# Hybrid encoder on one core: VectorE's order within an attention tile, the modulation's row sums in the mixer's tail, and the order of the first loads

## What is computed

```python
mod = silu(c) @ w_ada[l] + b_ada[l]                    # six vectors of 1024
h = rms_norm(x, norm1_g) * (1 + sc1) + sh1
za, zb, zq, zk, zv = split(h @ w_in)
ya = silu(rms_norm(depthwise_conv31(val(za) * sigmoid(gate(za))) + b))
yb = rms_norm(bg * depthwise_conv3(cg * hv))           # from zb
w = softmax(q1 k1) - lam * softmax(q2 k2);  yc = rms_norm(w @ v) * (1 - lambda_init)
x = x + g1 * (concat(ya, yb, yc) @ w_out)
h = rms_norm(x, norm2_g) * (1 + sc2) + sh2
x = x + g2 * (silu(h @ w_gate) * (h @ w_up)) @ w_down
```

## Time and profile before

| | |
|---|---|
| median of 3 runs | 1249.59 us (1248.78 to 1251.52) |
| the profiled execution's own time | 1248.77 us |
| its span in the trace | 1246.8 us |
| mean granted TensorE clock | 0.984 |
| PE busy | 1189.5 us, 95% |
| DVE busy | 730.5 us, 59% |
| ACT busy | 470.5 us, 38% |
| chain of waits, by engine | PE 70%, DVE 21%, ACT 4%, issue 4% |
| chain of waits, lines of VectorE | L908 (taps) 5%, L799 4%, L1004 1%, L989 1%, L844 1% |

### The profile page before, as it was taken

One profiled execution on the slowest core, in us unless ns is written; L12 is line 12 of the kernel. 1 busy time (PEld: TensorE's weight loads), 2 busy tenths in 40 slices (PEclk: granted clock), 3 DMA queues, 4 the chain that ended last, 5 costly groups with the idle time before them and its releaser, 6 DMA issues.

```text
span 1246.8 us, 14190 instructions
## 1 busy us (share of the span) xinstructions
PE 1189.5 (95%) x5080; PEld 926.1 (74%) x5080; DVE 730.5 (59%) x1032; ACT 470.5 (38%) x706; POOL 90.3 (7%) x163
## 2 busy tenths in 40 slices
PE   7999897969999999999989998989899999999998
PEld 5887543748888888888868875548688888888887
DVE  6889997886555533366665999645633333333331
ACT  5544657433332233322243345674422332232220
POOL 2402112201011000111000001000000000000000
PEclk9999998979999999999989999999999999999999
DMA  7742114655565322587422221203233223323332
GB/s 290 257 163 85 34 52 151 208 197 167 188 201 188 128 89 101 182 303 239 162 75 102 85 85 34 63 6 102 67 101 101 88 97 101 100 86 106 113 101 84
DMA packets 44328, 158.36 MB, mean 127 GB/s; under 512 B 5185, under 2 KB 5313, under 8 KB 44290
## 3 DMA queue, kind: packets, MB, share of 16 engines
q1 hardware_dynamic: 30386, 107.13, 25.5%
q0 software_dynamic: 13904, 50.73, 11.9%
HBM read 155.75 MB, written 2.10 MB: 127 GB/s over the span
## 4 chain that ended last, share of the span: by engine, by line
PE 70%; DVE 21%; ACT 4%; issue 4%; DMA 1%; POOL 0%; DVEq 0%; ACTq 0%; SPq 0%
PE ps L1234 20%; PE ps L1235 20%; PE ps L1236 20%; DVE uc L908 5%; DVE w_lo L799 4%; PE ps L1258 2%; DVE prob L1004 1%; PE ps L1442 1%; DVE neg_max L989 1%; DVE ada_ring_mid_b L844 1%; PE ps L1262 1%; DVE ta L975 1%; DVE tb L980 1%; DVE tn L970 1%; ACT prob L581 1%
## 5 line engine op out<-in xcount | busy, mean ns | idle before, releaser
L501 ACT ACTIVATE w_hi<-raw 128x1024 fp32r<-128x1024 f32 x196 | 207.8, 1060 | 577.2 <-PE ps L1236 492.5
L799 DVE TENSOR_TENSOR w_lo<-raw,w_hi 128x1024 fp32r<-128x1024 f32 x196 | 240.1, 1226 | 266.1 <-ACT w_hi L501 265.9
L1234 PE MATMUL ps<-h_hi,w_hi 128*128 128x512 f32 x848 | 334.4, 394 | 0.0
L1236 PE MATMUL ps<-h_lo,w_hi 128*128 128x512 f32 x848 | 330.4, 390 | 0.0
L1235 PE MATMUL ps<-h_hi,w_lo 128*128 128x512 f32 x848 | 330.2, 389 | 0.0
L1234 PEld LDWEIGHTS ps<-h_hi,w_hi 128*128 128x128 f32 x848 | 159.2, 188 | 48.2 <-issue 16.7
L1236 PEld LDWEIGHTS ps<-h_lo,w_hi 128*128 128x128 f32 x848 | 159.2, 188 | 33.4
L1235 PEld LDWEIGHTS ps<-h_hi,w_lo 128*128 128x128 f32 x848 | 159.3, 188 | 31.7
L1234 PE MATMUL ps<-gu_hi,w_hi 128*128 128x512 f32 x352 | 136.9, 389 | 0.0
L1235 PE MATMUL ps<-gu_hi,w_lo 128*128 128x512 f32 x352 | 136.9, 389 | 0.0
L1236 PE MATMUL ps<-gu_lo,w_hi 128*128 128x512 f32 x352 | 136.9, 389 | 0.0
(11 more groups left out here) (168 smaller groups left out, 1261.2 us busy)
## 6 DMA issues: line engine op xcount, KB each, us to landing
raw<-w_stream SPq DMA_DIRECT2D x196, 512.0 KB, 3.3
ada_ring_gu<-ada POOLq DMA_DIRECT2D x28, 512.0 KB, 4.3
ada_ring_late<-ada POOLq DMA_DIRECT2D x28, 512.0 KB, 4.9
ada_ring_first<-ada POOLq DMA_DIRECT2D x16, 512.0 KB, 5.8
ada_ring_mid_a<-ada POOLq DMA_DIRECT2D x12, 512.0 KB, 5.8
ada_ring_mid_b<-ada POOLq DMA_DIRECT2D x12, 512.0 KB, 4.9
xT<-x_t SPq DMA_DIRECT2D x4, 512.0 KB, 8.7
out_t<-xT SPq DMA_DIRECT2D x8, 256.0 KB, 4.3
```

The source lines that it names most:

```text
L501: act.activation(w_hi[:, u % RING, :], raw[:, u % RAW, :], ACT.Copy).then_inc(s_whi, 1)
L799: dve.tensor_tensor(w_lo[:, u % RING, :], raw[:, u % RAW, :], w_hi[:, u % RING, :].bitcast(F32), ALU.subtract).then_inc(s_wlo, 1)
L1234: pe.matmul(dst, whi, rhs[0][:, n, :], start=start, stop=False)
L1236: return pe.matmul(dst, whi, rhs[1][:, n, :], start=False, stop=stop)
```

## The change

VectorE's tile has another order: maxima of the next tile, mixing, one tap, the next tile's inverse, and then the other taps. Taps are given per tile and reach to tile 13 in both layers; the sums (50 and 26) are unchanged. In layer 0's tail the eight row sums 20 to 27 stand in pairs between the steps, where before four stood there and four behind; head 2's remainder (`y_lo(l, 3)`) is now ahead of the convolution's scaling (`mix_scale(l, 4)`), in both layers. GpSimd issues the loads 20 to 25 in pairs behind the factors of tiles 13, 14 and 15, where four came behind tile 13's and two behind tile 14's. At the start SyncE issues `pcol` after all of x, GpSimd's first two `ada` loads wait for the third load of x, ScalarE's first weight split comes ahead of the first gain, and VectorE's angle reduction and first weight remainder come ahead of the norm.

```diff
-TAPS_TILE = ([(1, 3)] * 10 + [(1, 4)] * 2, [(1, 3)] * 6 + [(2, 0)])
+TAPS_TILE = ((5, 4, 5, 3, 2, 4, 5, 3, 2, 3, 5, 3, 3, 3, 0, 0), (3, 2, 3, 1, 1, 2, 3, 1, 1, 1, 3, 1, 2, 2, 0, 0))
@@ SyncE
                 sp.dma_start(xT[:, 2 * i:2 * i + 2, :], x_in[:, 2 * i:2 * i + 2, :]).then_inc(s_x[i], 16)
-                if i == 1:
-                    sp.dma_start(pcol[:], pcol_in).then_inc(s_pc, 16)
+            sp.dma_start(pcol[:], pcol_in).then_inc(s_pc, 16)
@@ GpSimd, attention
-                    if l == 0 and it == N_TILES - 3:
+                    if l == 0 and it >= N_TILES - 3:
                         pool.wait_ge(s_scores, N_TILES)
-                        for m in range(M_MID + 4, M_MID + 8):
-                            ada_load(m)
-                    if l == 0 and it == N_TILES - 2:
-                        for m in range(M_MID + 8, M_MID + 10):
-                            pool.wait_ge(s_acc, m - 8 + 1)
+                        for m in range(M_MID + 2 * it - 22, M_MID + 2 * it - 20):
+                            if m >= M_MID + 8:
+                                pool.wait_ge(s_acc, m - 8 + 1)
                             ada_load(m)
@@ GpSimd, start
-            for m in range(2):
-                ada_load(m)
...
             pads()
+            pool.wait_ge(s_x[KC // 2 - 2], 16)
+            for m in range(2):
+                ada_load(m)
             pool.wait_ge(s_x[KC // 2 - 1], 16)
@@ ScalarE, start
             norm_rstd(0)
+            split_hi(0)
             act.wait_ge(s_pc, 16)
             act.wait_ge(s_n1b, 1)
             first_gain(0)
-            split_hi(0)
@@ VectorE, start
             angle_turns()
+            reduce_angles()
             dve.wait_ge(s_pc, 16)
...
             mod_dot(0)
             mod_dot(1)
-            reduce_angles()
+            split_lo(0)
             dve.wait_ge(s_nrs, 1)
...
                         norm_apply(0, 0, k)
-                        if k == 0:
-                            split_lo(0)
-                        elif k + 1 < KC:
+                        if k and k + 1 < KC:
                             mod_dot(2 * k + 2)
@@ VectorE, attention tile
-                    taps = TAPS_TILE[l][it] if it < len(TAPS_TILE[l]) else (0, 0)
-                    conv_a_taps(l, taps[0])
                     row_mix_in(l, it)
+                    taps = TAPS_TILE[l][it]
+                    conv_a_taps(l, min(taps, 1))
+                    if it + 1 < N_TILES:
+                        row_inverse(l, it + 1)
+                    conv_a_taps(l, taps - min(taps, 1))
                     if it in (3, 7):
                         short_input(l, it // 4)
                     if it in (9, 11):
                         short_gate(l, it // 2 - 4)
-                    conv_a_taps(l, taps[1])
-                    if it + 1 < N_TILES:
-                        row_inverse(l, it + 1)
@@ VectorE, tail
                 y_lo(l, 2)
-                mix_scale(l, 3)
-                mix_scale(l, 4)
-                y_lo(l, 3)
                 if l == 0:
                     for m in range(M_MID + 4, M_MID + 6):
                         mod_dot(m)
-                y_lo(l, 4)
+                mix_scale(l, 3)
                 if l == 0:
                     for m in range(M_MID + 6, M_MID + 8):
                         mod_dot(m)
+                y_lo(l, 3)
+                if l == 0:
+                    for m in range(M_MID + 8, M_MID + 10):
+                        mod_dot(m)
+                mix_scale(l, 4)
+                y_lo(l, 4)
+                if l == 0:
+                    for m in range(M_MID + 10, M_MID + 12):
+                        mod_dot(m)
                 mix_scale(l, 5)
                 y_lo(l, 5)
-                if l == 0:
-                    for m in range(M_MID + 8, M_MID + 12):
-                        mod_dot(m)
```

## The result

The changed kernel takes 1254.15 us (median of 15 runs, 1252.52 to 1258.77), the kernel before 1249.96 in as many. The ratio is 1.0035, with a 95% interval of 1.0027 to 1.0043: slower by 4.2 us by the medians (4.4 by the ratio), where +4.3 was forecast.

The account below looks back on a forecast made before the run. TensorE was taken to have most of the chain, VectorE the pace in four places. Terms 1.0 + 0 + 2.6 + 2.8 − 4.9 + 0.7 + 2.1 = +4.3 us on 1249.59 gave 1253.9, range 1249.0 to 1257.0.

Parts of the forecast that it names:

- start: First norm: the weight's first split and remainder delay the activations' remainder, +1.0 us, bounds 0 to +3.
- layer 0, tiles 0 to 11: Six taps fewer, −4.0 us, against twelve waits of 0.33 at the inverse, +4.0: sum 0.
- layer 0, tiles 12 and 13: Of three new taps one fits the inverse's wait, two lengthen each tile: +2.6 us.
- layer 0, tile 14: The mixing's 1.12 us wait for GpSimd goes, tile 15's inverse waits anyway: taken as 0, other end −1.1.
- layer 0, tail: Convolution's scaling held back, SiLU 4.4 us later, clock falls for 1.7; output units begin 2.8 us later.
- layer 1, tiles 0 to 11: Thinly spread taps leave TensorE's own pace of 4.51 or 5.35 us a tile: −4.9 us.
- layer 1, last tiles: Tile 12: one tap ahead of head 0's scaling, for which ScalarE waits, +0.7 us; tile 13 nothing.
- layer 1, tail: Convolution's scaling ends later than the SiLU's old start, all of it counting: +2.1 us.
- The second rival: Layer 0's tiles: no wait at the inverse, 14 × 0.33 us less; total −0.3, 1249.3 us; chance 0.13.
- The first rival: Both tails: scaling not held, row sums leave VectorE's path; total −3.9, 1245.7 us; chance 0.14.
- I take 0: Layer 1's tail: clock's price behind TensorE's gap of 3.0 us, left open at 0 to +1.7, taken as 0.
- the rivals of late loads and of the shared port: Start: first `ada` loads land late, perhaps by the port VectorE and GpSimd share; +6.3, 1255.9 us; chance 0.11.

Follow-up runs that it names:

- parts-together kernel: Changed kernel with start and tile order of before and the convolution's scaling ahead of head 2's remainder; new tap counts and row sums kept: 1240.24 us, ratio 0.9921.
- the second layer's taps alone: Kernel before with only the changed kernel's taps per tile in layer 1: 1246.58 us, ratio 0.9972.
- the new start alone: Kernel before with nothing but the changed kernel's start: 1250.66 us, ratio 1.0002.
- the tail's order undone: Changed kernel with the convolution's scaling again ahead of head 2's remainder, row sums left in the idle stretches: 1246.63 us, ratio 0.9975.
- the tile's order undone: Changed kernel with the order inside a tile of the kernel before, new tap counts kept: 1248.74 us, ratio 0.9989.
- the one with the early splits: Kernel with two taps ahead of the inverse, plus x loaded first and first weight splits ahead of the first rstd and row sums: 1239.91 us, ratio 0.9910.
- the kernel with fewer products of ones: As the one with the early splits, with 5 products of ones instead of 12 ahead of the statistics: 1239.57 us, ratio 0.9914.
- two taps ahead of the inverse: Parts-together kernel with mixing first, then two taps, the inverse, and the other taps: 1241.42 us, ratio 0.9922.

## Why the prediction came out right

The terms, as the prediction put them, beside the two profiled executions (each measured as a difference of two distances between the same events):

| term | forecast | measured |
|---|---|---|
| start | +1.0 | +0.98 at layer 0's first maxima |
| layer 0, tiles 0 to 11 | 0 | 0.0 |
| layer 0, tiles 12 and 13 | +2.6 | +2.65 |
| layer 0, tile 14 | 0 | −0.22 at the last mixing |
| layer 0, tail | +2.8 | +2.98 |
| layer 1, tiles 0 to 11 | −4.9 | −4.97 |
| layer 1, last tiles | +0.7 | +0.65 |
| layer 1, tail | +2.1 | +3.8 |
| sum | +4.3 | +5.9; the spans differ by 6.4 |

The last half microsecond lies outside these stages, 0.4 of it between layer 0's first addition to x and layer 1's first maxima. The medians' +4.2 against the forecast's +4.3 is closer than the terms deserve, and partly luck: the interval of the measured difference is 1 us either way, the start's 1.0 could not be found in the time, and in layer 1 the clock costs 1.6 in one execution and nothing in another, where the forecast had nothing.

**The tile's order.** Six taps fewer are −4.0, twelve waits +4.0: the one stands in the changed kernel, the other was taken away by itself and gave the 4.0 back. That the inverse can't come before 2.7 to 2.8 us is shown by tiles 0 to 2 above; with two taps ahead of it, at 3.12, it waits for nothing. The second rival (1249.3) is the time of the kernel without those waits, 1248.74.

**The last tiles.** Of the three taps one goes into the old wait and two lengthen each tile; two row sums there are part of what fills them, since without them the stretch is 1.68 shorter. Tile 14's wait for GpSimd (1.12 us in the earlier trace rows) is gone in the parts-together kernel too, which has the order of before and the loads in pairs; with the order of before and the loads of before it is 0.94 and 1.54 us (the second layer's taps alone; the new start alone). So the loads are what it waited for, or the counts of taps, which that kernel changes as well; the order of the mixing is not.

**Layer 0's tail.** The size of each piece was right: the SiLU later by 4.46 (forecast 4.4), TensorE's wait 5.37 (5.3), the clock's price 1.76 (1.7: SiLU to addition 12.46 us in the changed kernel, 10.70 with the scaling in its place), the row sums' 3.25 (3.3). In all three executions compared here the clock also fell at head 2's sum (1.58, 1.54 and 1.67 us long instead of 1.10), so that cancels. The first rival, that the tail works as it reads, was the right answer to another kernel, the one with the tail's order undone.

The Trainium skill, "TensorE: Matmul & The Clock Gate" (Part 1: The HAM clock gate), was cited for the long gap; the row from 231 to 237 with 0.50 agrees. The page also says that the point at which the clock rises differs from run to run, since the window over which activity is judged runs freely. The next paragraph's rows, equal waits with and without a fall, agree with such a spread; they don't show its cause.

**Layer 1's tail** is the term that was mis-sized: "I take 0" for the clock. The scaling's place cost 2.2 us there, as forecast (2.1); the other 1.6 are the clock, and in this execution it fell ahead of head 2's sum and not in the lengthened gap. It is a matter of the execution, not of the change: the kernel with nothing but the new start has the code of before in this tail and shows the fall at the same place, behind a gap of 2.37 us that the profile of before has too, without a fall.

```profile
832.30 5.17 PE L1440 MATMUL ps<-w_t,v 128*128 128x512 f32 x8
832.00:836.00 4.00, 4.00 (x6) 1.54 (x5) 0.75 (x1) 1.45 (x3) 0.00 (x0) 0.57 0.00 0
```

Eight products with v take 5.17 us there, and the granted clock is 0.57 over the stretch; in the profile of before they take 3.60 and the clock is 1.00. The record before the change already had such a fall, in layer 0, behind a still shorter wait; it is the second stretch of the earlier trace rows:

```profile
213.12 1.58 PE L1317 MATMUL ps<-work_b,ones 128*128 128x512 f32 x2 [1.99 <-ACT work_b L631]
```

"I take 0" for a wait of 3.0 us thus had a row against it.

The lengthened gap costs the clock in some executions as well: 3.09 us of idle time ahead of a sum of 1.10 us in the changed kernel, 3.10 ahead of one of 2.04 with the tile's order undone. The two profiled executions differ by 6.2 us in their own times and the medians by 4.2; the 1.6 of this fall would be most of that difference, but that isn't shown. Only a trace tells where the clock falls. Each run's mean clock is on record: 0.982 in 20 of 26 runs of the kernel before and 0.984 or 0.986 in the others, 0.974 to 0.981 in all 15 of the changed one. The profiled execution of before (0.984) thus had a higher clock than most of its kind.

**The start.** The 1.0 us is in the trace, for the reason given, but twice it could not be found in the time; it stays a local price. Two details were off: the second row sum was done at 18.0 us, not 19.4, since x landed in 5.7 us and not in 8.7; and of the rivals of late loads and of the shared port nothing is seen: the median of the 16 first `ada` loads is 6.1 us to landing beside 5.8. VectorE did wait 3.21 us for the first of them, until 15.61, but the norm's factor was not begun before 17.22.

## What to carry to other kernels

When idle stretches are filled, look at what each list item behind the filler releases on another engine: here a remainder that held nobody up stood ahead of a scaling for which ScalarE and then TensorE waited, and swapping the two turned 1254.15 us into 1246.63. An order that brings a result earlier gains nothing if its input isn't there: measure the distance from the event that starts the input (2.79 us here) and put as much work as it takes between. Where one engine is the pace only in some tiles, spread the movable work by tile until the other engine's period shows without gaps.

## What the runs showed of the hardware that was not expected

- Whether a gap of TensorE costs the clock isn't fixed by its length. Behind 1.99 us it fell in layer 0 of the kernel before and held in layer 1 with the tile's order undone; behind 2.37 us, in layer 1 with the same code, it fell in one execution and held in another; behind 3.10 it fell and behind 3.09 it held; behind 5.36 to 5.38 it fell in all three executions that have such a gap. Where it is down, the sum for a head takes up to 2.05 us instead of 1.10. One fall costs 1.4 to 1.8 us in the executions compared above; in the one with the early splits it cost 3.0 (14.29 us from head 2's sum to head 3's in layer 0, 11.25 in the kernel with fewer products of ones, the same code there).
- GpSimd's factor, one number for each of 128 partitions, takes 0.26 us ahead of tile 0, beside VectorE's reduction of maxima, and mostly 1.26 (0.69 to 1.27 in layer 0's tiles 0 to 12) when it is issued right behind the inverse with VectorE going on to taps. With two taps ahead of the inverse it took 2.40 in three tiles. Spans on GpSimd are rough:

```profile
127.20 1.26 POOL L408 TENSOR_SCALAR row_mix<-row_inv,neg_lam 128x1 f32<-128x1 f32 x1 [2.53 <-DVE row_inv L993]
124.41 0.26 POOL L408 TENSOR_SCALAR row_mix<-row_inv,neg_lam 128x1 f32<-128x1 f32 x1 [5.46 <-DVE row_inv L993]
```

The Trainium skill, "SBUF — State Buffer" ("SBUF: two separate sides"), describes a port pair of VectorE and GpSimd that one of them holds for a whole instruction. The longer of these rows would fit it, but 1.26 is longer than one tap (0.66), and no run here isolates the cause. The time is hidden here, as the mixing comes a maximum later.
